# Small products moved to the idle one of two projection banks, one to a visit, in a two-layer RWKV and attention block

## The reference, cut to what matters

```python
rz = hx @ w_in                      # split into conv, rwkv, gate and attention parts
zd = z + mu[d] * (shift_seq(z, offset) - z)             # d: forward, backward
r, k, v, lw, la = jnp.split(zd, RWKV_SPLITS, axis=-1)
w_log = -jax.nn.softplus(-(w0[d] + jnp.tanh(lw) @ w2[d])) - 0.5   # "decay"
a = jax.nn.sigmoid(a0[d] + la @ a2[d])                            # "rate"
kk = kk * lax.rsqrt(jnp.maximum(jnp.sum(kk * kk, axis=-1, keepdims=True), 1e-24))  # key norm
S = S * w[..., None, :] + sa[..., :, None] * b[..., None, :] + v[..., :, None] * k[..., None, :]
bonus = merge_dirs(jnp.sum(r * k * r_k, axis=-1, keepdims=True) * v)
y = (y - mean) * lax.rsqrt(var + LN_X_EPS) * heads(lnx_g) + heads(lnx_b) + bonus
return y * (jax.nn.sigmoid(lg) @ g2)
```

## Time and profile before

| | us |
|---|---|
| median of 3 runs | 3349.84 |
| lowest, highest | 3348.38, 3359.7 |
| the profiled execution | 3353.84 |
| its span | 3352.1 |
| granted TensorE clock, mean | 0.974 |

### The profile page before, as it was taken

How to read it: one execution, slowest core, us unless ns; L and a number is a source line. 1 busy time by engine, 2 the same in 40 slices (tenths; PEclk the granted TensorE clock), 3 DMA queues, 4 the chain that set the end, 5 groups by cost and what they waited for, 6 DMA issues and landing times.

```text
span 3352.1 us, 73768 instructions
## 1 busy us (share of the span) xinstructions
PE 3077.4 (92%) x31182; PEld 2446.6 (73%) x31182; DVE 1652.9 (49%) x3078; ACT 1163.3 (35%) x2403; POOL 827.8 (25%) x518
## 2 busy tenths in 40 slices
PE   7989898999999998999999888888899889989998
PEld 5767676777677786888888666666667667768886
DVE  4467585856444653100144465877676456330033
ACT  4433333433344424211112353443333345342222
POOL 2211111111123232222223221111111243434453
PEclk9999999999999999999999989999999999999999
DMA  5424243434454441111111233424143243522222
GB/s 209 135 91 145 84 132 114 129 123 143 145 173 149 154 169 57 51 63 63 63 50 63 75 97 99 120 66 123 60 128 107 92 141 123 180 69 96 98 88 75
DMA packets 246697, 363.76 MB, mean 109 GB/s; under 512 B 154080, under 2 KB 155376, under 8 KB 246160
## 3 DMA queue, kind: packets, MB, share of 16 engines
q1 hardware_dynamic: 226976, 294.57, 27.8%
q10 hardware_dynamic: 14976, 35.66, 2.7%
q0 software_dynamic: 4464, 29.46, 2.5%
HBM read 290.42 MB, written 69.21 MB: 107 GB/s over the span
## 4 chain that ended last, share of the span: by engine, by line
PE 70%; DVE 12%; issue 5%; ACT 4%; DVEq 3%; DMA 2%; POOLq 2%; SPq 1%; PEld 1%; POOL 0%; PEldq 0%; ACTq 0%
PE banks L281 19%; PE banks L282 17%; PE banks L283 17%; PE banks L1692 1%; PE banks L1684 1%; PE banks L1649 1%; PE banks L1024 1%; DVE arena L1810 1%; DVE arena L1837 1%; PE banks L395 1%; PE banks L1052 1%; DVEq L1833 1%; POOLq L2437 1%; PE banks L1742 1%; DVE arena L597 1%
## 5 line engine op out<-in xcount | busy, mean ns | idle before, releaser
L283 PE MATMUL banks<-hx_rounded,slot_rounded 128*128 128x512 f32 (+1 forms) x1624 | 576.9, 355 | 0.0
L907 POOL TENSOR_TENSOR slot_rounded<-slot,branch_weights_high 128x512 fp32r<-128x512 f32 x188 | 248.0, 1340 | 1286.2 <-ACT branch_weights_high L902 1284.8
L281 PE MATMUL banks<-hx_rounded,branch_weights_high 128*128 128x512 f32 (+1 forms) x1280 | 500.4, 391 | 53.2 <-DVE arena L1365 14.2
L281 PE MATMUL banks<-hx_high,weight_parts 128*128 128x512 f32 (+1 forms) x1512 | 538.1, 356 | 10.9 <-DVE hx_low L545 10.4
L282 PE MATMUL banks<-hx_low,weight_parts 128*128 128x512 f32 (+1 forms) x1512 | 538.2, 356 | 0.0
L283 PE MATMUL banks<-hx_high,weight_parts 128*128 128x512 f32 (+1 forms) x1512 | 536.5, 355 | 0.0
L282 PE MATMUL banks<-resid_rounded,branch_weights_high 128*128 128x512 f32 (+1 forms) x1280 | 455.1, 356 | 0.0
L283 PEld LDWEIGHTS banks<-hx_rounded,slot_rounded 128*128 128x128 f32 x1624 | 314.0, 193 | 44.3
L281 PEld LDWEIGHTS banks<-hx_rounded,branch_weights_high 128*128 128x128 f32 x1280 | 247.4, 193 | 134.0 <-issue 83.1
L281 PEld LDWEIGHTS banks<-hx_high,weight_parts 128*128 128x128 f32 x1512 | 287.0, 190 | 55.1 <-issue 13.9
L283 PEld LDWEIGHTS banks<-hx_high,weight_parts 128*128 128x128 f32 x1512 | 286.3, 189 | 40.9
(11 more groups left out here) (263 smaller groups left out, 5861.6 us busy)
## 6 DMA issues: line engine op xcount, KB each, us to landing
slot<-in_w_mix SPq DMA_DIRECT2D x120, 512.0 KB, 3.9
slot<-in_w_ffn_in SPq DMA_DIRECT2D x88, 512.0 KB, 3.7
arena<-chunk_inputs SPq DMA_DIRECT2D x48, 640.0 KB, 4.7
arena<-in_w_ada SPq DMA_DIRECT2D x50, 512.0 KB, 5.1
slot<-in_w_ffn_out SPq DMA_DIRECT2D x44, 512.0 KB, 3.6
slot<-in_w_ada SPq DMA_DIRECT2D x40, 512.0 KB, 4.1
chunk_inputs<-arena SPq DMA_DIRECT2D x80, 256.0 KB, 3.9
arena<-side_projections POOLq DMA_DIRECT2D x16, 1152.0 KB, 6.2
```

The costliest lines, as they stand in the source:

```text
L281: first = nc.tensor.matmul(out, w_hi, x_hi, start=start, stop=False)
L283: return first, nc.tensor.matmul(out, w_lo, x_hi, start=False, stop=stop)
L907: last = nc.gpsimd.tensor_tensor(slots_r[g % 3][:, half], slots[g % 3][:, half], weights_high(g)[:, half], ALU.subtract)
```

## The change

What it does, by parts:

- The small products leave the list of the tiles. A second generator, `smalls()`, gives them out, and `one_small()` takes at most one of them in a visit, right behind the chain's products of that visit and ahead of the filler. In the prologue they become due by the tile that is in work (`reach`), in a body stage by a number of visits since the last one (`reach_gap`).
- A small product goes to the bank that the tile in work does not fill (`1 - at_bank.filling`), and its reader takes it from there (`place_of`). None is given out when the tile segment in work has just ended (`left` is 0).
- All tiles have the order [0, 1]. `tile_bank` is as it was.
- ScalarE rounds the weights of tile t + 2 when the first segment of tile t ends, which is now s=0 where a tile has it. Its preparation and readout threads now stand ahead of the evictions.
- VectorE's steps follow the new visits. The formulas for their distances are as before, but for the readers of small products, which have one visit for each segment. The products and their number are the same.

The core of the diff (the same edit of a reader is shown once):

```diff
         def tile_order(g):
 
             st, _, t = TILES[g]
-            return [0, 1] if (st, t) in ((BODY, 8), (TAIL, 5)) else [1, 0]
+            return [0, 1]
...
             def small(name, s, lhs, rhs, done, taken_by, count=1):
-                at_bank.free(s)
-                nc.tensor.matmul(pair(6)[s], lhs, rhs, start=True, stop=True).then_inc(done.sem, count)
-                at_bank.busy[s] = taken_by
-                mark(name)
-                return COST[s] * 1.25
+                b = 1 - at_bank.filling
+                at_bank.free(b)
+                place = place_of[l, st, hp, name, s] = bank[6 + b][:, 0:SEGS[s][1] - SEGS[s][0]]
+                nc.tensor.matmul(place, lhs, rhs, start=True, stop=True).then_inc(done.sem, count)
+                at_bank.busy[b] = taken_by
+                mark((name, s))
+                last_small[0] = where[0]
+                filler.spent += COST[s] * 1.25
...
+            def tiles():
+                first = 0
                 if st == PRO:
                     for s in tile_order(0):
                         at_bank.busy[tile_bank(l, 0, s)] = (seg_taken[s], seg_count(l, 0, s))
                         mark((0, s))
                     at_bank.slot_before = 0
-                    yield from tile(1)
+                    first = 1
+                for t in range(first, TILES_IN[st]):
+                    if (st, t) == (TAIL, 5):
+                        while where[0] < VISITS[TAIL]:
+                            yield None
+                    for s in range(2):
+                        at_tile[0] = (t, s)
+                        yield from tile(t, s)
+
+            def reach(t, s):
+                while at_tile[0] < (t, s) and not last_call[0]:
+                    yield
+
+            def reach_gap(gap):
+                while where[0] < gap and not last_call[0]:
+                    yield
...
                 elif st == BODY:
                     yield from decay_and_rate(0)
-                    yield from tile(0, 1)
+                    yield from reach_gap(last_small[0] + 2)
                     yield from key_norm(0)
-                    yield from tile(0, 0)
-                    yield from tile(1, 1)
-                    yield from tile(1, 0)
+                    yield from reach_gap(last_small[0] + 5)
                     yield from bonus_sum(0)
-                    yield from tile(2, 1)
+                    yield from reach_gap(last_small[0] + 2)
                     yield from decay_and_rate(1)
-                    yield from tile(2, 0)
-                    yield from tile(3, 1)
+                    yield from reach_gap(last_small[0] + 2)
                     yield from key_norm(1)
-                    yield from tile(3, 0)
-                    yield from tile(4, 1)
+                    yield from reach_gap(last_small[0] + 3)
                     yield from bonus_sum(1)
-                    yield from tile(4, 0)
-                    yield from tile(5)
+                    yield from reach_gap(last_small[0] + 4)
+                if st != PRO:
+                    if st == TAIL:
+                        yield from reach(4, 1)
                     yield from gate_of_readout()
...
+                    yield from reach_gap(LAST_OF_HEAD + 1 if st == BODY else VISITS[TAIL])
                     yield from sum_of_readout(0)
...
+                    yield from reach_gap(last_small[0] + 2)
                     yield from sum_of_readout(1)
...
+            def one_small():
+                if at_bank.left:
+                    next(smalls_left, None)
...
             for v in range(VISITS[st]):
                 chain.visit()
                 where[0] = FREE[st] + v
+                one_small()
                 filler.upto(free + busy * sum(shares[:v + 1]) / sum(shares))
...
             filler.upto(1e9)
+            last_call[0] = True
+            for _ in smalls_left:
+                pass
...
             def rounding():
                 for g in range(g0 + 2, g0 + nt + 2):
-                    yield at((g - 2, 1))
+                    yield at((g - 2, 0 if 0 in tile_segs(l, g - 2) else 1))
                     tile_round(act, l, g)
...
-            threads = [Thread(eviction())] + ([Thread(preparation())] if st != TAIL else []) + ([Thread(readout())] if st != PRO else []) + [Thread(rounding())]
+            threads = ([Thread(preparation())] if st != TAIL else []) + ([Thread(readout())] if st != PRO else []) + [Thread(eviction()), Thread(rounding())]
...
-                    assert g < at(("norm", d)), (st, hp, d, g, at(("norm", d)))
-                    g = at(("norm", d))
-                    yield g
-                    for i, s in enumerate(sum_order(l, st)):
+                    assert g < at((("norm", d), 1)), (st, hp, d, g, at((("norm", d), 1)))
+                    for i, s in enumerate((1, 0)):
+                        g = at((("norm", d), s))
+                        yield g
                         dve.wait_ge(pre_prod.sem, pre_prod.ready(l, hq, k + 5 + i))
-                        nc.vector.tensor_scalar(TMP[6][:, TSEG[s][0]:TSEG[s][1]], pair(6)[s], 1e-24, None, ALU.max).then_inc(pre_dve.sem, 1)
+                        nc.vector.tensor_scalar(TMP[6][:, TSEG[s][0]:TSEG[s][1]], place_of[l, st, hp, ("norm", d), s], 1e-24, None, ALU.max).then_inc(pre_dve.sem, 1)
```

More of the change, by code:

```diff
@@ L838, in __init__ @@
                 self.pe, self.busy, self.slot_before = pe, [None, None], None
+                self.filling, self.left = 0, 1
             def free(self, s):
@@ L1047, in decay_and_rate @@
                     pe.wait_ge(small_full, (l * (HP + 1) + stage) * 16 + 16 if st == PRO else hp * 16 + (l * (HP + 1) + 2) * 16)
-                for i, s in enumerate((1, 0)):
[L1049 to L1056, removed]
@@ L1058, in key_norm @@
-            def key_norm(d):
-                for i, s in enumerate(sum_order(l, st)):
+                for n, (s, x) in enumerate(((1, 0), (1, 1), (0, 0), (0, 1))):
+                    r = slice(64 * x, 64 * x + 64)
+                    small(("both", d, x), s, SMALL[r, d * P:(d + 1) * P], LD[r, d, SEGS[s][0]:SEGS[s][1]], pre_prod, (pre_act.sem, pre_act.ready(l, hq, 8 * d + n + 1)))
+                    if n == 3 and d == 1 and st == PRO:
+                        nc.tensor.drain().then_inc(small_free.sem, 1)
+                    yield
@@ L1095, in steps @@
                     yield from decay_and_rate(1)
-                    nc.tensor.drain().then_inc(small_free.sem, 1)
-                    yield from tile(5)
+                    yield from reach(5, 1)
                     yield from key_norm(1)
-                    yield from tile(6)
+                    yield from reach(6, 1)
                     yield from bonus_sum(1)
-                    for t in range(7, 11):
-                        yield from tile(t)
                 elif st == BODY:
                     yield from decay_and_rate(0)
-                    yield from tile(0, 1)
+                    yield from reach_gap(last_small[0] + 2)
@@ L1123, in steps @@
-                    yield from tile(7)
-                    while where[0] <= LAST_OF_HEAD:
-                        yield None
+                    yield from reach_gap(LAST_OF_HEAD + 1 if st == BODY else VISITS[TAIL])
                     yield from sum_of_readout(0)
-                    summed = where[0]
-                    yield from tile(8, 0)
-                    while where[0] <= summed:
-                        yield None
+                    yield from reach_gap(last_small[0] + 2)
                     yield from sum_of_readout(1)
-                    yield from tile(8, 1)
-                else:
-                    for t in range(4):
-                        yield from tile(t)
-                    yield from gate_of_readout()
-                    yield from tile(4)
-                    while where[0] < VISITS[TAIL]:
-                        yield None
-                    yield from sum_of_readout(0)
-                    yield from tile(5, 0)
-                    yield from sum_of_readout(1)
-                    yield from tile(5, 1)
+            smalls_left = smalls()
@@ L1149, in stage_pe @@
             prep, read = 4 * 1.25 * sum(COST) + 2 * 1.25 * out_cost, 3 * 1.25 * out_cost
-            filler = Filler(steps())
+            filler = Filler(tiles())
             shares = [SHARE[(chain.visits + v) % PERIOD] for v in range(VISITS[st])]
```

87 lines of the change are left out of this document (48 added, 39 removed).

## The result

The changed kernel takes 3456.85 us (median of 4 runs, 3454.43 to 3460.09) against 3351.82 us (4 runs) of the kernel before on the same chip: ratio 1.0311, 95% interval 1.0289 to 1.0332. It is slower, as forecast, but by 105 us and not by 40; the range ended at 3420.

The account below looks back on a forecast made before the run. TensorE, busy 92% of the span, was taken to bound the kernel, with 72.5 us of bank waits to win. 88 us added less 48 taken: 40 over 3353.8 us, itself 4.0 over the median, so 3390 us; range 3350 to 3420.

Parts of the forecast that it names:

- How the visits shift: Body stage of layer 0: small products spread over later visits; direction 0's last input moves from visit 11 to 15.
- (a): Layer 0's body stages, visit 15: the fifth block's load comes late and TensorE stands 8.2 us a stage, 25 us.
- (b): Layer 0's body stages: tile 5's weights load late, ScalarE's sigmoid and a row product wait; 8 us a stage, 24 us.
- (c): Layer 0's body stages: the load for the next pair's first block lands late, 3.4 us a stage, 10 us.
- (d): End of layer 0's stages: TensorE waits for both banks at the readout; 1.7 us a stage, 5 us.
- (e), layer 1: Layer 1's body stages: late chunk loads, 6.2 us in the first, 3.5 each in the others; sum 16.6 us.
- (e), the prologues: Prologues start their first block's load three and four visits later, visits of about 1 us: 7 us, could be 2.
- The clock ... at nothing.: TensorE's half-speed stretches behind new stalls set against old ones that go: nothing added, 25 us kept above the sum.
- Rival 1: TensorE's clock falls after every new stall and no old slow stretch goes: 40 + 25, about 3415 us; chance 0.2.
- I take two thirds, 48 us: TensorE's waits for small-product readers and tiles in banks 6 and 7: 48 us of the 72.5 us go.
- the pool: Eight rows of TensorE's waits for readers of small products and tiles in banks 6 and 7, 72.5 us.

Follow-up runs that it names:

- experiment 1: Changed kernel with the fifth block's chunk inputs loaded ahead of direction 0's three stores in body stages of both layers: 3399.62 us, ratio 1.0121 to the kernel before.
- experiment 5: Kernel before, with only the fifth block's load in layer 0's body stages issued later, behind the row write and a store: 3383.4 us, ratio 1.0077.
- experiment 2: Changed kernel with tile 5's weights loaded ahead of the store of direction 1's first input: 3431.94 us, ratio 1.0221 to the kernel before.
- experiment 3: Changed kernel with both queue edits, the fifth block's load and tile 5's weights issued earlier: 3375.91 us, ratio 1.0046 to the kernel before.
- experiment 6: Changed kernel, queue order kept, with ScalarE rounding a weight tile behind the second segment, half a tile later than either kernel: 3430.78 us, ratio 1.0221.
- Experiments 7 and 8: Changed kernel with both loads issued first and the prologue's decay and rate products two (7) or three (8) visits apart: 3358.07 and 3358.15 us, ratios 1.0001 and 1.0005.
- experiment 4: Experiment 3's kernel with the prologue's direction 1 decay-and-rate and key norm products due one tile segment later: 3371.01 us, ratio 1.004 to the kernel before.
- experiments 10 and 11: Layer 0 as before; layer 1 as experiment 7, both loads first (10), in 11 with its old prologue too: 3343.93 and 3340.32 us, ratios 0.9953 and 0.9944.
- experiment 9: Experiment 7's kernel with the bodies' direction 0 bonus sum and direction 1 key norm one visit later: 3418.36 us, ratio 1.0174 to the kernel before.

## Why the prediction was right in direction and wrong in size

- **"How the visits shift" and (a).** Right, shift and mechanism. The fifth block waited 9.1, 8.5 and 8.8 us in layer 0's three stages; the sum said 8.2. Its place and its releaser are those named, and experiments 1 and 5 show it from both sides.
- **(b).** The mechanism is right. The wait is larger, 10.6 us in the second stage for 8 predicted, but 7.7 us of it come back as another wait: 31 us by experiment 2 and 24 by experiments 1 and 3, for 24. "Rounds them at visit 17, before and after" is right, and so is the sigmoid queued behind it: it moved from visit 13 to 18. Experiment 6 shows that this order on ScalarE is as much a cause as the late load.
- **(c).** Right in kind, 1.0 to 1.5 us a stage for 3.4. **(d)**: at the end of each stage of layer 0 the chain waits 2.0 us for an eviction, where it waited 1.7 us for the row reader: 0.3 us a stage for 1.7.
- **(e), layer 1.** 5.7, 4.1 and 4.0 us at the fifth blocks for 6.2, 3.5 and 3.5.
- **All chunk waits together.** 64.9 - 11.2 = 53.7 us, where (a), (c) and (e) without the prologues said 25 + 10 + 16.6 = 51.6.
- **(e), the prologues.** The first term that failed. "Visits without a chain, of about 1 us": 7 us taken, 16.3 + 3.5 in layer 0 and 12.1 in layer 1 measured, 32 us. I had counted how much later the load is issued, and not what one product to a visit does in visits this short. Experiments 7 and 8 show that this placing is part of it, and experiment 4 excludes the store; 10.7 us in layer 0 stay unexplained, and experiment 6 won 6.6 us there by rounding later, so more than one cause is at work.
- **"The clock ... at nothing."** The step that failed most: I set the new slow stretches against the old ones. The busy time grew by 52.3 us. By stage 19.4 us of it lie in layer 0's body stages, 12.3 in layer 1's, 15.2 in the two prologues with their first blocks, the rest elsewhere. Rival 1 had the mechanism, with 25 us for it: ten stalls at up to 2.5 us. Experiment 1 measures 24.4 us less busy time in the body stages with six of these stalls gone, so about 4 us each. The windows of the changed kernel say why it is more: behind (a) the clock is 0.50 and 0.54 in two windows of 5 us, where I had counted one. The earlier trace rows end at 209; the next window of the kernel before shows that the stretch was as long there:

```profile
209.00:214.00 5.00, 4.66 (x16) 3.03 (x18) 0.00 (x0) 3.02 (x5) 0.00 (x0) 0.54 0.00 0
```

  But one price does not fit: experiment 5 gives 1 to 3 us a stall. And the 15.2 us of the prologues stand behind no stall for a transfer of this size; the sum had no clock there at all.

  The Trainium skill, "TensorE: Matmul & The Clock Gate", section "HAM oscillation — how this bites in real kernels", describes a kernel in which each wait for a transfer leaves the next stretch cold. The trace agrees behind the long waits (0.50 behind those of 8.51 and 10.60 us) and not behind the short one of 1.31 us, where the clock is 1.00. For the long ones I should have let this rule decide over my setting new stretches against old ones.
- **"I take two thirds, 48 us."** Too much. Of the 72.5 us some 37 are left in the same kinds of row, and row products, which never waited for these readers before, wait some 16 for them ((b) left out): about 20 us taken. In layer 0's bodies it is nothing net (16.6 to 15.9), in layer 1 it is real, but late loads and a longer prologue covered it (experiments 10 and 11). The list of visits had shown the row products ("or a row product, follows a small product into its bank"); I priced them as shortened waits, and they are new ones.

The sum by parts: idle time, forecast +40, measured +54, with the prologues too low and the pool too high; busy time, forecast 0, measured +52.

## What to carry to other kernels

When work is re-spaced on one engine, list every transfer that an order written by hand puts behind its results, and ask which load has come to stand behind a store that is now later: one issue moved on the queue was worth 63 of 105 us. Do the same for each engine that takes its work in order: a reader that moves behind a step that waits for a load inherits the wait. Add to each new stall the slow stretch behind it, with a price from this kernel's rows (here 1 to 5 us), and do not net it against old ones. Give a change that helps one stage to that stage alone: here it wins in layer 1's body stages, where no row products share the bank, and costs in the prologues.

## What I had not expected

- The same kind of stall had different prices: about 5 us of slow products behind each in layer 0 of the changed kernel (experiment 1), 1 to 3 us in the kernel before (experiment 5).
- Removing (b), with 10.6 us of waiting and a clock of 0.50 behind it, did not lower the busy time when the load came earlier (3129.7 and 3132.5 us), and lowered it to 3118.6 us when the rounding came later, at the same total time. Why is left open.
- Idle time need not come from a long wait to cost clock: in the prologue no single wait of TensorE was above 3.6 us, and the granted clock was 0.62 and 0.74 over 18 and 20 us, where it had been 0.81 and 1.00.
- A shift by one visit of a few small products cost some 60 us (experiment 9), more than half of what the whole change had cost.
